# A decoder layer's start: modulation in matching chunks, index projections block by block, small loads moved

## The reference, cut to what matters

```
mod = silu(c) @ w_ada + b_ada                   # 6 * 1024 columns
shift_a, scale_a, gate_a, shift_m, scale_m, gate_m = split(mod, 6)
h = rms_norm(x, g_attn) * (1 + scale_a) + shift_a
proj = h @ w_in                                  # latent, index queries and key, attention q, k, v
```

## Time and profile before

| what | value |
|---|---|
| median of 3 runs (lowest, highest) | 1076.32 us (1075.5, 1076.68) |
| the profiled execution: time | 1077.77 us |
| its span | 1075.8 us |
| PE busy | 947.4 us, 88% |
| DVE busy | 599.7 us, 56% |
| ACT busy | 400.7 us, 37% |
| POOL busy | 113.7 us, 11% |

### The profile page before, as it was taken

The page is one execution under the profiler, slowest core; times in us unless marked ns, Lnnn a source line. Parts: engine busy times, 40 slices in busy tenths (PEclk is TensorE's granted clock), DMA queues, the critical chain, the costliest instruction groups (busy, mean ns, idle before and its releaser), DMA issues.

```text
span 1075.8 us, 14803 instructions
## 1 busy us (share of the span) xinstructions
PE 947.4 (88%) x5250; PEld 513.1 (48%) x5250; DVE 599.7 (56%) x1567; ACT 400.7 (37%) x902; POOL 113.7 (11%) x212
## 2 busy tenths in 40 slices
PE   1899999999999799878999899999499999979920
PEld 1446476444448567555666555555233433323400
DVE  2387436999999487768676414346423322312238
ACT  4302035676740277766667512122112111201102
POOL 2100000000008300110000000000111111111002
PEclk9899999999999899989999899999599999989975
DMA  9994100110111000012000221156889999999977
GB/s 333 366 338 172 40 20 20 40 39 21 40 40 26 1 1 1 1 66 113 2 2 1 101 96 58 79 232 240 344 341 423 420 416 421 421 420 421 394 309 299
DMA packets 65755, 191.43 MB, mean 178 GB/s; under 512 B 10184, under 2 KB 27904, under 8 KB 53392
## 3 DMA queue, kind: packets, MB, share of 16 engines
q1 hardware_dynamic: 56544, 172.35, 41.5%
q0 software_dynamic: 5760, 16.78, 3.9%
q10 hardware_dynamic: 3376, 1.33, 0.5%
HBM read 172.60 MB, written 22.04 MB: 181 GB/s over the span
## 4 chain that ended last, share of the span: by engine, by line
PE 80%; DMA 6%; DVE 6%; issue 4%; ACT 3%; ACTq 1%; SPq 0%; DVEq 0%; POOL 0%; POOLq 0%
PE PS L1583 15%; PE PS L1883 12%; PE PS L1768 11%; PE PS L1685 6%; PE PS L1906 6%; PE PS L1706 4%; PE PS L1728 3%; PE PS L1630 3%; DMA SC<-in_w_up_dram 3%; PE PS L1562 3%; PE PS L1592 3%; PE PS L1723 3%; PE PS L1870 2%; PE PS L1607 2%; PE PS L1575 1%
## 5 line engine op out<-in xcount | busy, mean ns | idle before, releaser
L1583 PE MATMUL PS<-HT,X 128*128 128x512 f32 x384 | 168.8, 593 | 0.0
L1883 PE MATMUL PS<-QKV,HT 128*32 128x512 f32 (+2 forms) x640 | 132.1, 614 | 3.4 <-DMA SC<-in_w_up_dram 1.7
L839 ACT ACTIVATE X<-X,nmx 128x896 f32<-128x896 f32 (+7 forms) x128 | 98.6, 772 | 68.0 <-DVE nmx L1153 67.6
L1768 PE MATMUL PS<-QKV,HT 128*128 128x512 f32 x256 | 116.7, 610 | 0.0
L1583 PEld LDWEIGHTS PS<-HT,X 128*128 128x128 f32 x384 | 72.5, 190 | 92.4 <-issue 92.2
L1089 DVE TENSOR_SCALAR_CACHE_REDUCE BIAS<-SC,tk 128x384 f32<-128x384 f32 (+3 forms) x128 | 96.4, 809 | 1.1
L1685 PE MATMUL PS<-QKV 64*128 64x512 f32 (+3 forms) x384 | 83.2, 539 | 10.9 <-DVE nmx L1153 10.1
L1437 DVE TENSOR_TENSOR HT<-PS,HT 128x256 f32<-128x256 f32 x20 | 8.5, 425 | 144.8 <-ACT HT L937 144.8
L816 ACT ACTIVATE X<-SC,tk 128x896 f32<-128x896 f32 x64 | 69.6, 1088 | 43.1 <-DVE tk L1077 43.1
L1768 PEld LDWEIGHTS PS<-QKV,HT 128*128 128x128 f32 x256 | 48.5, 195 | 55.6 <-issue 55.5
L1153 DVE CUSTOM_DVE_ANT_0 X<-PS,R 128x256 f32<-128x256 f32 (+7 forms) x80 | 51.0, 675 | 32.2 <-PE PS L1685 31.8
(11 more groups left out here) (281 smaller groups left out, 1448.5 us busy)
## 6 DMA issues: line engine op xcount, KB each, us to landing
QKV<-in_w_ada_dram SPq DMA_DIRECT2D x12, 2048.0 KB, 14.6
QKV<-in_w_gate_dram SPq DMA_DIRECT2D x22, 1024.0 KB
QKV<-in_w_up_dram SPq DMA_DIRECT2D x22, 1024.0 KB
QKV<-in_w_down_dram SPq DMA_DIRECT2D x22, 1024.0 KB, 27.1
X<-in_w_in_dram SPq DMA_DIRECT2D x16, 512.0 KB, 3.8
QKV<-expert_rows SPq DMA_DIRECT2D x16, 512.0 KB, 10.3
X<-in_w_gate_dram SPq DMA_DIRECT2D x5, 1024.0 KB
X<-in_w_up_dram SPq DMA_DIRECT2D x5, 1024.0 KB
```

What stands on the lines that cost most here:

```text
L839: act.activation(sc, sc, ACT.Exp, bias=nmx[:, i % 4, m:m + 1], scale=-1.0, accum_out=rs[:, i, m:m + 1]).then_inc(exp_done, 1)
L1583: end = pe.matmul(PS[:, 2 * b + half, :], WS[:, b, j, :], HT[:, j, BANK * half:BANK * (half + 1)], start=(j == 0), stop=(j == KC - 1))
L1768: end = pe.matmul(PS[:, n % 4, :], HT[:, k, P * (n // 2):P * (n // 2 + 1)], wo[:, k, BANK * (n % 2):BANK * (n % 2 + 1)], start=(k == 0), s ...
L1883: end = pe.matmul(PS[at, 2 + b, :], hgT[b][:, P * c_ + at.start:P * c_ + at.stop], WGU[w][:, c_, :, :], start=(c_ == 0), stop=(c_ == KC - 1))
```

## The change

- A chunk i of the first four now holds 256 columns of shift_a and the 256 matching columns of scale_a, in two loads with rows of 1 KB (`ada_pair`); so chunk i gives mod and sc1 for blocks 2 i and 2 i + 1. WI is loaded behind the first chunk instead of behind the fourth.
- After each chunk VectorE forms its part of mod and sc1, and the two blocks are made at once. ScalarE makes blocks 3, 5 and 7.
- The index products run over j outside and n inside: each block j goes into all four products, in four banks. `ada_part(1..3)` and `ada_cols(1..3)` stand between the blocks.
- Four of the sixteen copies of turned groups (9, 11, 13, 15) go to VectorE. The second half of the turning is split around `ada_cols(0)`.
- Row 0 stands behind the index products, rows 1 to 3 ahead of latent tiles 2, 4 and 6, row 4 to 7 where they were.
- Eight small loads (L737 to L745) go to the head of ScalarE's queue, w_uk and w_uv behind its blocks of h, on a semaphore of their own shared with the final gain.
- `x2_done` is dropped; who waited for it waits for `x2_half`.

```diff
-        aff_on_act = (2, 5)
+        aff_on_act = (3, 5, 7)
+        xt_on_dve = (9, 11, 13, 15)
...
+            def ada_pair(i):
+                for a in range(2):
+                    sp.dma_start(ada[i][:, :, 2 * P * a:2 * P * (a + 1)],
+                                 w_ada[0, :, D * a + 2 * P * i:D * a + 2 * P * (i + 1)].rearrange("(j p) n -> p j n", p=P)
+                                 ).then_inc(ada_in[i], 16)
...
             for i in range(4):
-                ada_load(i)
-            sp.dma_start(WI, win_d[:, :, OFF_LAT:OFF_FQ]).then_inc(wi_in, 16)
+                ada_pair(i)
+                if i == 0:
+                    sp.dma_start(WI, win_d[:, :, OFF_LAT:OFF_FQ]).then_inc(wi_in, 16)
...
         def _(act):
+            act.dma_start(gkv[:, :], g_kv.partition_broadcast(P).rearrange("p o n -> p (o n)")).then_inc(small_in, 16)
...
             act.wait_ge(cols_sb, 1)
...
-            act.dma_start(wuk[:, :, :], w_uk[0].rearrange("h c d -> c h d")).then_inc(small_in, 16)
-            act.dma_start(wuv[:, :, :], w_uv[0].rearrange("h c d -> c h d")).then_inc(small_in, 16)
             for g in range(2 * KC):
                 half, j = g // KC, g % KC
-                act.wait_ge(xt_ps, g + 1)
-                act.activation(HT[:, j, BANK * half:BANK * (half + 1)], PS[:, g % 4, :], ACT.Copy).then_inc(xt_act, 1)
+                if g not in xt_on_dve:
+                    act.wait_ge(xt_ps, g + 1)
+                    act.activation(HT[:, j, BANK * half:BANK * (half + 1)], PS[:, g % 4, :], ACT.Copy).then_inc(xt_act, 1)
...
             for j in aff_on_act:
+                act.wait_ge(mod_done, 2 * (j // 2) + 2)
                 act.activation(HT[:, j, :], HT[:, j, :], ACT.Identity, bias=mod[:, j:j + 1], scale=sc1[:, j:j + 1]
                                ).then_inc(aff_act, 1)
+            act.dma_start(wuk[:, :, :], w_uk[0].rearrange("h c d -> c h d")).then_inc(act_in, 16)
+            act.dma_start(wuv[:, :, :], w_uv[0].rearrange("h c d -> c h d")).then_inc(act_in, 16)
...
+            def keep_x(g):
+                dve.wait_ge(xt_ps, g + 1)
+                dve.tensor_copy(HT[:, g % KC, BANK * (g // KC):BANK * (g // KC + 1)], PS[:, g % 4, :]).then_inc(xt_dve, 1)
+
+            for i in range(4):
+                if i == 0:
+                    for g in xt_on_dve[:2]:
+                        keep_x(g)
+                keep_sums(i)
+                if i == 0:
+                    for g in xt_on_dve[2:]:
+                        keep_x(g)
+                a, b = slice(2 * i, 2 * i + 2), slice(KC + 2 * i, KC + 2 * i + 2)
+                dve.wait_ge(ada_done, i + 1)
+                dve.tensor_tensor(mod[:, a], PS[:, 7, 4 * i:4 * i + 2], cols[:, a], ALU.add).then_inc(mod_done, 1)
...
+                for j in (2 * i, 2 * i + 1):
+                    if j not in aff_on_act:
+                        dve.tensor_scalar(HT[:, j, :], HT[:, j, :], sc1[:, j:j + 1], mod[:, j:j + 1], ALU.mult, ALU.add
+                                          ).then_inc(aff_dve, 1)
...
-            turn_x(0)
+            turn_x(0, range(KC))
             pe.wait_ge(cact_done, 1)
             ada_part(0)
-            turn_x(1)
+            turn_x(1, range(4))
             ada_cols(0)
-            for b in range(1, 4):
-                ada_part(b)
-                ada_cols(b)
+            turn_x(1, range(4, KC))
...
+            for j in range(KC):
+                if j in aff_on_act:
+                    pe.wait_ge(aff_act, aff_on_act.index(j) + 1)
+                else:
+                    pe.wait_ge(aff_dve, j + 1 - sum(a < j for a in aff_on_act))
+                for n in range(4):
                     end = pe.matmul(PS[:, n, :], WI[:, j, LAT:LAT + P] if n < 2 else WIK[:, j, :],
                                      HT[:, j, BANK * (n % 2):BANK * (n % 2 + 1)], start=(j == 0), stop=(j == KC - 1))
...
+                if 1 <= j < 4:
+                    ada_cols(j)
+                if j < 3:
+                    ada_part(j + 1)
+            ada_row(0)
...
             for t in range(T):
-                if t == 3:
-                    ada_row(3)
+                if t in (2, 4, 6):
+                    ada_row(t // 2)
...
-                    pe.wait_ge(x2_done, q + 1)
+                    pe.wait_ge(x2_half, 2 * q + 2)
```

More of the change, by code:

```diff
@@ L318, in hybrid_layer @@
         part_ps, part_sb, wgr_in = sem("part_ps"), sem("part_sb"), sem("wgr_in")
-        aff_on_act = (2, 5)
+        aff_on_act = (3, 5, 7)
+        xt_on_dve = (9, 11, 13, 15)
+        xt_dve = sem("xt_dve")
         wcopy = sem("wcopy")
@@ L333, in hybrid_layer @@
             sem(n) for n in ("o_square", "o_rstd", "o_done", "ot_done", "ot_copied", "half_copied"))
-        wo_in, gf_in = sem("wo_in"), sem("gf_in")
-        op_ps, x2_done, x2_sq, x2_rstd, h2_done = (
-            sem(n) for n in ("op_ps", "x2_done", "x2_sq", "x2_rstd", "h2_done"))
+        wo_in, act_in = sem("wo_in"), sem("act_in")
+        op_ps, x2_sq, x2_rstd, h2_done = (
+            sem(n) for n in ("op_ps", "x2_sq", "x2_rstd", "h2_done"))
         h2_out = [sem(f"h2_out{i}") for i in range(2)]
@@ L514, in _ @@
                         down_load(sp, expert_of(w), w)
-                sp.wait_ge(x2_done, t + 1)
+                sp.wait_ge(x2_half, 2 * t + 2)
                 sp.dma_start(x2_dram[P * t:P * (t + 1), :], XT[:, t, :]).then_inc(x2_out, 16)
@@ L729, in _ @@
         def _(act):
[L730 to L736, removed]
             act.dma_start(gkv[:, :], g_kv.partition_broadcast(P).rearrange("p o n -> p (o n)")).then_inc(small_in, 16)
@@ L745, in _ @@
                           ).then_inc(small_in, 16)
-            act.dma_start(wuk[:, :, :], w_uk[0].rearrange("h c d -> c h d")).then_inc(small_in, 16)
-            act.dma_start(wuv[:, :, :], w_uv[0].rearrange("h c d -> c h d")).then_inc(small_in, 16)
+            act.wait_ge(cols_sb, 1)
+            act.activation(cexp[:, :], cols[:, MODC:MODC + KC], ACT.Exp, scale=-1.0).then_inc(cexp_done, 1)
+            for t in range(T):
+                act.wait_ge(x_in[t // 2], 16)
+                if t:
+                    act.wait_ge(sq_done, t)
+                act.activation(BIAS[:, 2, :], XT[:, t, :], ACT.Square, accum_out=ss[:, t:t + 1]).then_inc(sq_done, 1)
             for g in range(2 * KC):
                 half, j = g // KC, g % KC
-                act.wait_ge(xt_ps, g + 1)
-                act.activation(HT[:, j, BANK * half:BANK * (half + 1)], PS[:, g % 4, :], ACT.Copy).then_inc(xt_act, 1)
-            act.wait_ge(xt_act, 2 * KC)
-            act.wait_ge(mod_done, 2)
+                if g not in xt_on_dve:
+                    act.wait_ge(xt_ps, g + 1)
+                    act.activation(HT[:, j, BANK * half:BANK * (half + 1)], PS[:, g % 4, :], ACT.Copy).then_inc(xt_act, 1)
+            act.wait_ge(xt_act, 2 * KC - len(xt_on_dve))
+            act.wait_ge(xt_dve, len(xt_on_dve))
             for j in aff_on_act:
+                act.wait_ge(mod_done, 2 * (j // 2) + 2)
                 act.activation(HT[:, j, :], HT[:, j, :], ACT.Identity, bias=mod[:, j:j + 1], scale=sc1[:, j:j + 1]
                                ).then_inc(aff_act, 1)
+            act.dma_start(wuk[:, :, :], w_uk[0].rearrange("h c d -> c h d")).then_inc(act_in, 16)
+            act.dma_start(wuv[:, :, :], w_uv[0].rearrange("h c d -> c h d")).then_inc(act_in, 16)
             act.wait_ge(lam_ready, 2)
@@ L900, in _ @@
             for t in range(T):
-                act.wait_ge(x2_done, t + 1)
+                act.wait_ge(x2_half, 2 * t + 2)
                 if t:
@@ L963, in _ @@
                             ev_h(n, over(b))
-            act.dma_start(gfin, g_final.partition_broadcast(P)).then_inc(gf_in, 16)
+            act.dma_start(gfin, g_final.partition_broadcast(P)).then_inc(act_in, 16)
             for t in range(T):
@@ L1010, in keep_row, with keep_sums @@
                                   ).then_inc(arow_sb, 1)
-            for i in range(4):
+            def keep_sums(i):
                 dve.wait_ge(part_ps, i + 1)
@@ L1016, in _ @@
                 dve.tensor_copy(halfsum[i % 2], PS[:, 4 + i % 2, :]).then_inc(part_sb, 1)
[L1018 to L1029, removed]
+            def keep_x(g):
[12 more added lines that the diff above has]
+                dve.tensor_tensor(mod[:, a], PS[:, 7, 4 * i:4 * i + 2], cols[:, a], ALU.add).then_inc(mod_done, 1)
+                link(dve.tensor_tensor(sc1[:, a], PS[:, 7, 4 * i + 2:4 * i + 4], cols[:, b], ALU.add))
+                dve.tensor_tensor(sc1[:, a], sc1[:, a], cols[:, MODC + KC + 2 * i:MODC + KC + 2 * i + 2], ALU.mult
+                                  ).then_inc(mod_done, 1)
+                dve.wait_ge(mod_done, 2 * i + 2)
+                if i == 0:
+                    dve.wait_ge(xt_act, 2 * KC - len(xt_on_dve))
+                    dve.wait_ge(xt_dve, len(xt_on_dve))
+                for j in (2 * i, 2 * i + 1):
+                    if j not in aff_on_act:
```

(38 more changed lines are left out.)

## The result

The changed kernel runs in **1067.68 us** (median of 5), the kernel before in 1075.5 us on the same chip: ratio of their times 0.9925 (95% interval 0.9909 to 0.994). One of the five executions was slow (1178.06 us at a granted clock of 0.824 against 0.956 in the others); it is in the median, not in the ratio. A second reading gave 1068.47 against 1075.76 us, ratio 0.9944 (0.9922 to 0.9965); two of its eleven executions of the changed kernel took 1077 us, the others 1066.6 to 1069.6. The forecast was 1069.2 us and a gain of 7.1 us; measured are 7.8 and 7.3 by the medians, 8 and 6 by the ratios.

A forecast was written before the change was run, and what follows sets the result against it. TensorE's queue was taken to bound the kernel. The fourth slab projection ending at 123.0 instead of 130.46 us gives 7.4, less 0.3 for semaphore steps: 7.1 us gained, so 1069.2 us, 8 in 10 within 1065.5 to 1073.5.

The forecast's parts named there:

- fourth slab projection ends: End of the stretch the change touches: TensorE finishes this projection at 123.0 us instead of 130.46.
- x held up by the small loads: Load of x at the start: small loads' packets going out beside it delay it 0.6 us, at most 1.2.
- first eight groups: TensorE's first transposes: four groups at the slow rate 3.67 us, four at the fast 1.82, from 17.0 to 22.5.
- wait for VectorE's copies: After group 11, before the first chunk's columns: TensorE waits 1.4 us for two VectorE copies of 0.69.
- wait for the first block: After the last transposes: TensorE waits 2.1 us while VectorE finishes group 15, small operations and the first block.
- a chunk in rows of 1 KB: Loads of w_ada: one chunk takes 6.0 us, within 5.4 to 7.1.
- chunks 1 to 3 hidden: Index block loop: these chunks land at 31, 37, 43 us, before TensorE asks at 36.1, 42.6, 49.1.
- first to last index matmul: Index products with parts and columns between them: from 32.6 to 69.7 us on TensorE.
- rows 3 and 4 wait: Row products after the index products: TensorE waits for VectorE's row sums, 0.5 us at row 3, 2.1 at row 4.
- Rival A: Start, around the two waits before the first block: clock falls again, 1.7 to 2 us given back, 1071.1 us; chance 0.17.
- Rival C: Index block loop: stop and go keeps the clock low, kernel slower, 1083 to 1097 us; chance 0.07.
- Rival D: Row products: slower sums make rows 0 to 4 7 us later, gain given back, 1076.3 us; chance 0.07.

The follow-up runs named there:

- E11: Changed kernel with only two of the eight small loads at the head of ScalarE's queue, six behind its copies of turned groups: 1067.29 us in one execution.
- E12: Changed kernel with all eight small loads in SyncE's queue, behind x and ahead of w_ada: 1070.83 us in one execution.
- E2: Changed kernel with the eight small loads behind ScalarE's copies of the turned groups instead of at its queue's head: 1065.58 us, ratio 0.9912 to the kernel before.
- E3: Changed kernel with row products 4, 5, 6 one slab projection later and row 7 behind row 6: 1066.86 us, ratio 0.9913 to the kernel before.
- E4: Changed kernel with both the small loads behind ScalarE's copies and the later row products: 1064.53 us, ratio 0.9893 to the kernel before.
- E6: Changed kernel with the load moves undone, all ten small loads back behind the squares of x: 1073.21 us, ratio 0.9966 to the kernel before.
- E7: Changed kernel with parts and columns of chunks 1 to 3 ahead of the index products, these one after the other: 1079.67 us, ratio 1.0024 to the kernel before.
- E8: Kernel before with only x2_done replaced by the counts of halves: 1076.4 against 1076.56 us, ratio 0.9994.
- E5: Kernel before with only the load moves and the waits that go with them: 1073.75 us, ratio 0.9969.

## Why the prediction was right, point by point

The time, the sign and the mechanism were right: TensorE's holes at the start close, the new ones are where they were expected, and the gain at the fourth slab projection is kept. That the time came out a little better than forecast, though the fourth slab projection ends 1.45 us later than forecast, is luck: the kernel before ends it at 131.3 us in the mean of three executions, not at 130.46, and what lies behind it scatters by some us (939.9 to 945.3), and the prediction has neither. By its own steps:

| step | forecast | measured |
|---|---|---|
| x held up by the small loads | 0.6 (0 to 1.2) | 3.0 |
| first transposes | 17.0 | 19.43 |
| first eight groups | 5.5 | 5.23 |
| wait for VectorE's copies | 1.4 | 1.38 |
| wait for the first block | 2.1 | 2.05 |
| a chunk in rows of 1 KB | 6.0 us | 349 GB/s: 6.0 us |
| chunks 1 to 3 hidden | yes | no wait |
| first to last index matmul | 37.1 | 36.3 |
| rows 3 and 4 wait | 0.5, 2.1 | 0.25, 1.99 |
| fourth slab projection ends | 123.0 | 124.45 |

- **The step that was mis-sized** is the first, "at most 1.2 us": 1024 packets at 18.5 ns. That price is the time in which a packet keeps a data engine busy. E11 and E12 show that small loads take longer than that while the engines are half idle (share 0.35 to 0.45 in the changed kernel and E12); what makes them slow stays open. E2 shows the whole 3.1 us coming back. The rule of the Trainium skill (Trainium Kernel Development and Optimization, section Key Constraints), that loads from SP and ACT share the 16 engines, pointed the right way: x is 3.0 us late. But the sum that the prediction made by it, 0.6 us worse, was still too small, and with engines half idle their sharing alone does not explain the delay.
- **Where the 2.4 us went.** The kernel lost them at the start against the forecast; 0.3 came back ahead of the first block and 0.8 in the index products, where a part took 1.86 from start to start instead of 1.95 and the columns 0.85 instead of 1.0; 0.2 was lost again behind, which left 1.45 at 124.45.
- **Rows.** The wait of row 4 in front of the slab projections was right to 0.1 us; E3 and E4 price it, with the new place of the rows, at 2.0 to 2.4.
- **Rival A** (the clock falls between the two holes) is real: of the eight profiled executions with these two holes and the block order it is there in two, E3 (3.4 us) and E6 (2.3), and in neither of the changed kernel. Its price was added up wrongly: four matmuls at 1.76 instead of 0.88 are 3.5 us, not 1.7 to 2. **Rival C** did not happen in the block order; E7 shows something like it in the other one: holes between the parts, a low clock behind them, slower than before. **Rival D**: no, rows 0 to 4 waited 2.2 us in all.
- **The total.** The front gives 6.7 us (131.3, the mean of three fourth ends, less 124.6, the mean of two). The readings of the time are 8 and 6 with about 2 us of uncertainty each, so the front explains it. Whether the 2 to 3 us that the profiled executions of before are longer behind the fourth end belong to the change stays open: E8 finds nothing of the half counts within 2.2 us, and no other edit touches the order of the work there.

## What to carry to other kernels

Follow the queue of the engine that bounds a stage and write its holes down one by one: here two edits that are worth 0.3% each add up to about 0.6%, and what either leaves behind alone can be read in its trace, as the next wait of TensorE (E5, E6). When work is reordered to hide a transfer, the margin to ask for is that between landing and use (3.5 to 3.8 us here), and the work that fills it also kept the clock up (E7, where it is missing). Small loads do not belong ahead of or beside a large one that the start waits for: behind the copies, where nothing is waiting, the same eight loads cost nothing that the fourth end shows (E2).

## What the runs showed that was not expected

Eight loads of some 270 KB in all held a 4 MB load up by 3.0 us from another queue, and the next load by 5 us in the same queue, with the data engines at a share of 0.35 to 0.45 for 2 to 4 us. And executions differ by up to 4 us in the attentions, where neither the work nor its order differs (248.7 to 252.9 us over all kernels here, 250.7 to 252.9 over three executions of the kernel before); an effect of 1 to 2 us is seen in the stage's own rows long before it is seen in the time.
